# A decoder block on one core: orders of the FFN opening and of the last norm, and two held GpSimd splits

## What is computed

```python
for i in range(DEPTH):                      # DEPTH is 1
    a = rmsnorm(h, ln_mix[i])
    z = a @ w_in[i]                         # q, k, v, output gate, low-rank gate, u
    ...                                     # o: chunked gated linear attention, y_pool: trailing means
    mix = jnp.concatenate([o, y_pool], axis=-1) @ w_out[i]
    h = h + mix
    f = rmsnorm(h, ln_ffn[i])
    h = h + (jax.nn.silu(f @ w_ffn_gate[i]) * (f @ w_ffn_up[i])) @ w_ffn_down[i]
    e = rmsnorm(h, ln_ple[i])
    h = h + jax.nn.sigmoid(e @ w_ple_gate[i]) * (p[i].astype(h.dtype) @ w_ple_proj[i])
return rmsnorm(h, ln_final)
```

## Time and profile before

| | us |
|---|---|
| three timed runs | 1169.32, 1170.78 (median), 1171.07 |
| the profiled execution | 1169.47 |
| its span, first to last instruction | 1167.2 |
| TensorE busy | 1138.9 (98%) |
| VectorE, GpSimd, ScalarE busy | 642.6, 567.9, 405.5 |
| mean granted TensorE clock | 0.988 |

### The profile page before, as it was taken

The page is one execution under the profiler, slowest core; times in us unless marked ns, Lnnn a source line. Parts: engine busy times, 40 slices in busy tenths (PEclk is TensorE's granted clock), DMA queues, the critical chain, the costliest instruction groups (busy, mean ns, idle before and its releaser), DMA issues.

```text
span 1167.2 us, 15072 instructions
## 1 busy us (share of the span) xinstructions
PE 1138.9 (98%) x5614; PEld 943.4 (81%) x5614; DVE 642.6 (55%) x753; ACT 405.5 (35%) x635; POOL 567.9 (49%) x368
## 2 busy tenths in 40 slices
PE   9999999999999899999999999999999999999995
PEld 7788998777887688888888888888888888778884
DVE  7565576557548764445454545454545353884434
ACT  8402112164324442323233333333332332473422
POOL 0011275233226876656665656565656565782203
PEclk9999999999999999999999999999999999999997
DMA  6211111113001111111111111111111110401003
GB/s 246 90 36 37 37 38 37 36 73 144 37 1 36 54 56 54 54 54 54 54 54 54 54 54 54 54 54 54 54 54 54 54 54 18 180 1 45 10 1 144
DMA packets 23364, 67.94 MB, mean 58 GB/s; under 512 B 2528, under 2 KB 3616, under 8 KB 21408
## 3 DMA queue, kind: packets, MB, share of 16 engines
q1 hardware_dynamic: 23328, 67.44, 16.3%
HBM read 63.24 MB, written 4.19 MB: 58 GB/s over the span
## 4 chain that ended last, share of the span: by engine, by line
PE 36%; POOL 31%; issue 23%; DVE 5%; DMA 2%; ACT 1%; POOLq 1%; SPq 0%; DVEq 0%; ACTq 0%
POOL r_lo L553 18%; PE pb L1494 10%; PE pb L1495 10%; PE pb L1496 10%; POOL raw_b L571 4%; POOL raw_a L569 3%; POOL s_sum L564 2%; POOL raw_a L567 2%; PE pb L1621 2%; DVE t_raw L1307 1%; PE pb L1605 1%; POOL sums L613 1%; PE pb L1582 1%; DMA pp_raw<-in_w_ple_proj_dram 1%; PE pb L1567 1%
## 5 line engine op out<-in xcount | busy, mean ns | idle before, releaser
L1373 DVE TENSOR_TENSOR h<-h,pb 128x512 f32<-128x512 f32 x176 | 116.9, 682 | 51.9 <-PE pb L1496 50.8
L553 POOL TENSOR_TENSOR r_lo<-raw_b,r_hi 128x512 fp32r<-128x512 f32 x66 | 96.0, 1455 | 100.5 <-ACT r_hi L766 100.5
L489 POOL TENSOR_TENSOR w_lo<-w_raw,w_hi 128x2048 fp32r<-128x2048 f32 x10 | 49.8, 4981 | 183.1 <-ACT w_hi L630 183.1
L1717 PE MATMUL pb<-t_hi,r_hi 128*128 128x512 f32 x352 | 137.5, 391 | 0.0
L1718 PE MATMUL pb<-t_lo,r_hi 128*128 128x512 f32 x352 | 137.0, 389 | 0.0
L1719 PE MATMUL pb<-t_hi,r_lo 128*128 128x512 f32 x352 | 136.9, 389 | 0.0
L553 POOL TENSOR_TENSOR r_lo<-raw_a,r_hi 128x512 fp32r<-128x512 f32 x66 | 89.9, 1363 | 94.1 <-ACT r_hi L766 94.1
L1494 PE MATMUL pb<-gu_hi,r_hi 128*128 128x512 f32 x320 | 124.5, 389 | 0.0
L1495 PE MATMUL pb<-gu_lo,r_hi 128*128 128x512 f32 x320 | 124.5, 389 | 0.0
L1496 PE MATMUL pb<-gu_hi,r_lo 128*128 128x512 f32 x320 | 124.5, 389 | 0.0
L766 ACT CAST r_hi<-raw_b 128x512 fp32r<-128x512 f32 x66 | 41.0, 622 | 203.3 <-POOL raw_b L571 143.9
(11 more groups left out here) (219 smaller groups left out, 2627.7 us busy)
## 6 DMA issues: line engine op xcount, KB each, us to landing
raw_d<-in_w_ffn_down_dram SPq DMA_DIRECT2D x22, 512.0 KB, 3.5
w_raw<-in_w_in_dram SPq DMA_DIRECT2D x7, 1024.0 KB, 4.9
raw_a<-in_w_ffn_gate_dram SPq DMA_DIRECT2D x11, 512.0 KB, 3.4
raw_b<-in_w_ffn_gate_dram SPq DMA_DIRECT2D x11, 512.0 KB, 4.4
raw_a<-in_w_ffn_up_dram SPq DMA_DIRECT2D x11, 512.0 KB, 3.7
raw_b<-in_w_ffn_up_dram SPq DMA_DIRECT2D x11, 512.0 KB, 4.6
h<-in_x_t_dram SPq DMA_DIRECT2D x16, 256.0 KB, 6.0
w_raw<-in_w_out_dram SPq DMA_DIRECT2D x4, 1024.0 KB, 5.8
```

Of the source, the lines that this page charges most:

```text
L489: nc.gpsimd.tensor_tensor(w_lo[s][:, 0:size], w_raw[s][:, 0:size], w_hi[s][:, 0:size].bitcast(F32), ALU.subtract).then_inc(w_lo_ready[s], 1)
L553: nc.gpsimd.tensor_tensor(r_lo[q % RING][:].rearrange("p (k n) -> p k n", k=kts), src, r_hi[q % RING][:].bitcast(F32).rearrange("p (k n) - ...
L1373: V.tensor_tensor(h[:, m, both(c)], h[:, m, both(c)], aux.bank(F_DOWN + n)[:], ALU.add).then_inc(aux.drained, 1)
L1717: M(bank[:], wh[:, k, :], x_h[:, k, :], start=start and k == 0, stop=False, skip_group_check=True)
```

## The change

- **GpSimd in the output projection**: the split of the first w_out block now waits for four o_tok scalings, that of the second for eight o_low splits.
- **Buffers and loads of the opening**: the first up matrix is loaded as four quarters (`up21`, `up22`, `up11`, `up12`) in places of their own, three of them before the output projection ends. up21 and up22 lie where rms_all is, so VectorE's copies into rms_all wait for the 14th split.
- **Orders in the opening**, on ScalarE, GpSimd and VectorE. The spreading of the norm stands behind P9, one product earlier.
- **PLE**: GpSimd's first gate split waits for the last gu_lo; the casts and splits of the first w_ple_proj block and of p stand between the tiles of the e row.
- **Last norm**: the half 0 sums, root and spread stand inside the last two gate products; GpSimd multiplies m = 4 to 7 of half 0 and m = 6, 7 of half 1, from copies that ScalarE makes, VectorE the others from PSUM; TensorE does 14 matmuls of ones before the last sums and spreads half 1 to two banks; table loads of ScalarE are called ahead by dummy activations; the stores go in another order.

The core of the diff:

```diff
+        up21, up22 = (at(n, [P, HK, P], small[0] + o * KB) for n, o in (("up21", 0), ("up22", 2)))
...
             matrix_half(w_ffn_gate, 0, 1, raw_b, b_landed, (w_lo_ready[1], 5))
-            sp.wait_ge(ent_lo, 3)
-            matrix_half(w_ffn_up, 0, 0, raw_a0, a_landed, (proj.filled, U_OUT + 16))
-            matrix_half(w_ffn_up, 0, 1, raw_b0, b_landed, (proj.filled, U_OUT + 16))
+            def up_quarter(dst, half, right, landed):
+                part = w_ffn_up[0][:, half * HK * BW:(half + 1) * HK * BW].rearrange("p (k n) -> p k n", k=HK)
+                sp.dma_start(dst[:], part[:, :, right * P:(right + 1) * P]).then_inc(landed, 16)
+
+            sp.wait_ge(proj.drained, U_OUT)
+            up_quarter(up21, 0, 1, up2_landed)
+            up_quarter(up22, 1, 1, up2_landed)
+            sp.wait_ge(proj.filled, U_OUT + 12)
+            up_quarter(up11, 0, 0, up11_landed)
+            sp.wait_ge(proj.filled, U_OUT + 16)
+            up_quarter(up12, 1, 0, up12_landed)
             for i in range(1, GROUPS):
...
-            for c, normed in enumerate((y_first, y_second)):
-                for k in range(KT):
-                    sp.wait_ge(normed, k + 1)
+            for k in (0, 4, 1, 2, 5, 3, 6, 7):
+                sp.wait_ge(*((y_first, k + 1) if k < 4 else (y_first_pool, k - 3)))
+                sp.dma_start(out[k][:, both(0)], h[:, k, both(0)]).then_inc(out_stored, 16)
+            for c, normed in ((1, y_second),):
+                for k in (0, 1, 2, 3, 6, 4, 5, 7):
+                    sp.wait_ge(*((normed, k + 1) if k < 6 else (y_second_pool, k - 5)))
...
+            pool.wait_ge(o_scaled, 4)
             block_lo(NB)
...
+            pool.wait_ge(o_lo, 8)
             for b in range(NB + 1, NB + 4):
                 block_lo(b)
...
+            opening_lo(0)
+            pool.wait_ge(b_landed, 16)
+            opening_sum(0, 0)
+            opening_sum(0, 1)
+            opening_lo(1, 2)
+            opening_sum(0, 2)
+            opening_sum(0, 3)
+            opening_lo(3, 4)
+            pool.wait_ge(up2_landed, 32)
+            opening_sum(1, 0)
+            opening_sum(1, 1)
+            opening_sum(1, 2)
+            opening_lo(5, 6)
+            opening_sum(1, 3)
+            opening_lo(*range(7, D_FIRST))
             with pool.Fori(0, GROUPS - 1) as d:
...
+            pool.wait_ge(gu_lo_ready, 2 * GROUPS)
             gate_lo(0)
-            proj_lo(0)
-            pool.wait_ge(gu_ready, 2 * GROUPS)
...
             for n in range(16):
+                if n == 2:
+                    proj_lo(0)
+                if n in (4, 6):
+                    k = n // 2 - 2
+                    pool.wait_ge(p_hi_done, k + 1)
+                    nc.gpsimd.tensor_tensor(p_lo[:, k, :], p_raw[:, k, :], p_hi[:, k, :].bitcast(F32), ALU.subtract
+                                            ).then_inc(p_lo_done, 1)
...
-            pool.wait_ge(aux.drained, F_NORM4 + 2)
             pool.wait_ge(h_gained, 14)
-            for m in range(KT):
+            pool.wait_ge(spread_copied, 1)
+            for m in range(4, KT):
                 nc.gpsimd.tensor_tensor(h[:, m, both(0)], h[:, m, both(0)], rms_all[:, both(0)], ALU.mult
-                                        ).then_inc(y_first, 1)
+                                        ).then_inc(y_first_pool, 1)
+            pool.wait_ge(h_gained, 16)
+            pool.wait_ge(spread_copied, 2)
+            for m in range(6, KT):
+                nc.gpsimd.tensor_tensor(h[:, m, both(1)], h[:, m, both(1)], rms_all[:, both(1)], ALU.mult
+                                        ).then_inc(y_second_pool, 1)
...
-            proj_high(0, ent_lo, END + 4)
...
             for n in range(16):
+                if n == 2:
+                    proj_high(0, ent_lo, END + 4)
+                if n in (4, 6):
+                    k = n // 2 - 2
+                    act.wait_ge(p_landed, 16)
+                    act.wait_ge(aux.filled, F_NORM3 - 16)
+                    nc.scalar.copy(p_hi[:, k, :], p_raw[:, k, :]).then_inc(p_hi_done, 1)
...
+                if pair == 7:
+                    nc.scalar.activation(stat[:, 2, 1:2], ones[:, 0:1], ACT.Sqrt)
+                    root(3, 0)
+                    nc.scalar.activation(stat[:, 2, 2:3], ones[:, 0:1], ACT.Sigmoid)
                 for n in ns:
+                    if n == 15:
+                        act.wait_ge(aux.filled, F_NORM4 + 2)
+                        nc.scalar.copy(rms_all[:, both(0)], aux.bank(F_NORM4 + 1)[:]).then_inc(spread_copied, 1)
...
             root(3, 1)
+            act.wait_ge(aux.filled, F_NORM4 + NORM_FILLS + 1)
+            nc.scalar.copy(rms_all[:, both(1)], aux.bank(F_NORM4)[:]).then_inc(spread_copied, 1)
...
+                if pair == 7:
+                    norm_var(F_NORM4, 0)
+                    norm_diag(3, 0)
...
                     if n == 14:
-                        norm_var(F_NORM4, 0)
-                        norm_diag(3, 0)
-                if pair == 7:
-                    norm_take(F_NORM4, 0)
+                        dve.wait_ge(spread_copied, 1)
+                        dve.wait_ge(h_gained, 14)
+                        for m in range(4):
+                            i = V.tensor_tensor(h[:, m, both(0)], h[:, m, both(0)], aux.bank(F_NORM4 + 1)[:], ALU.mult
+                                                ).then_inc(y_first, 1)
...
-            for m in range(KT):
+            for m in range(6):
...
-                    if (mat, idx) == (0, 6):
+                    if (mat, idx) == (0, 5):
...
 
+            def last_sums(k):
+                if k == 5:
+                    token_sums(F_NORM4, 0, (y_sum, 14))
+
+            def last_spread(k):
+                if k == 3:
+                    spread_rms(F_NORM4, 3, 0)
+
...
             f = F_NORM4 + 2
+            aux.claim(f + 1)
+            for _ in range(LAST_ONES):
+                M(aux.bank(f + 1)[:, 0:P], ones[:], ones[:], start=True, stop=True)
             pe.wait_ge(y_sum, 15)
-            aux.claim(f)
+            pe.wait_ge(aux.drained, F_NORM4)
...
-            aux.claim(f + 1)
-            for t in range(4):
-                i = M(aux.bank(f + 1)[:, t * P:(t + 1) * P], stat[:, 3, 4 + t:5 + t].broadcast_to([P, P]), ident[:],
-                      start=True, stop=True)
-            i.then_inc(aux.filled, 1)
+            for bank in (aux.bank(f + 1), aux.bank(f + 2)):
+                for t in range(4):
+                    i = M(bank[:, t * P:(t + 1) * P], stat[:, 3, 4 + t:5 + t].broadcast_to([P, P]), ident[:],
+                          start=True, stop=True)
+                i.then_inc(aux.filled, 1)
```

162 lines of the change are left out of this document (84 added, 78 removed).

## The result

The changed kernel takes **1162.38 us** (median of four runs, 1161.71 to 1163.34), the kernel before in the same series 1170.92; ratio 0.9925, 95% interval 0.9911 to 0.9939. The forecast was 1156.6 with a range of 1152 to 1162: faster, as said, but 7.8 us by the profiled executions (1169.47 and 1161.71) instead of 14.2. Most of the difference arises in one place.

What follows compares the result with a forecast made beforehand. TensorE, busy 98% of the span, was taken as the bound, with 16 us of waits in four places. Gains of 2.3 + 7.0 + 0 + 4.9 = 14.2 turn 1169.47 into 1155.3, forecast as a 1156.6 median; range 1152 to 1162.

Steps and rivals of the forecast that it cites:

- Part 1: Output projection: o_tok scalings no longer blocked by GpSimd, part of the gain lost to later waits; 2.3 us gained.
- the one of 0.3: Output projection: second new TensorE wait, for an o_low split behind the second mix_lo instruction; 0.3 us.
- The lock rule: A GpSimd instruction blocks VectorE instructions with both sources in SBUF for its whole length; projection gain 2.3 us.
- a shared bandwidth: Alternative reading of GpSimd and VectorE sharing SBUF access in the output projection; the gain there would be 3.3 us.
- Part 2: FFN opening: three TensorE waits and slow clock go, smaller VectorE waits come; 7.0 us gained, bounds 2.5 and 10.4.
- a wait of 1.4 at the diagonal: FFN opening: TensorE waits 1.4 us for VectorE's diagonal product before spreading the norm.
- P17's weights are ready by 408.7 at the latest and wanted at 410.2: Fourth loop product: GpSimd's split delivers its weights before TensorE wants them, so no wait there.
- Part 3: Last down projection and PLE splits: 0 us, from -0.7 to +1.5.
- nothing: Last down projection: the wait for the last gu_lo moves the first gate split only from 1006.67 to 1006.96.
- Part 4: Last norm: fewer GpSimd multiplications, ones keeping the clock up, faster sums and spread; 4.9 us gained, bounds 1.2 and 5.5.
- opening slower: FFN opening: VectorE 1 to 3 us later, or clock down at P10; gain 9 to 12, about 1160; chance 0.24.
- slower than before: Around the first silu: casts, copies and GpSimd's sums all late behind one scaling, eating the 14 us; chance 0.06.

Runs made afterwards that it cites:

- o_lo_hold_off: The changed kernel without GpSimd's wait for the eighth o_low split ahead of its splits of w_out blocks 2 to 4; 1165.62 us.
- no_ones: The changed kernel without the 14 matmuls of ones before the last token sums; 1165.91 us.
- before_again: The kernel before, unchanged, in a second execution; 1169.28 us.
- gu_hold_off: The changed kernel without the one line that makes GpSimd's first PLE gate split wait for VectorE's last gu_lo split; 1168.96 us.
- gu_casts_later: The changed kernel with the two gu_hi casts of each loop pass moved on ScalarE behind the copies of the first two products; 1158.89 us.

## Why the forecast missed, part by part

**Part 1 was right**: 2.56 by A, forecast 2.3. The rows of the changed kernel, VectorE's first o_tok scalings and o_low splits, and TensorE's transposes and first w_out product:

```profile
252.95 2.50 DVE L1277 TENSOR_TENSOR o_tok<-o_tok,o_stat 128x512 f32<-128x512 f32 x4
...
262.89 4.16 DVE L1283 TENSOR_TENSOR mix_lo<-gated,mix_hi 128x512 fp32r<-128x512 f32 x4
...
256.96 1.91 PE L1653 MATMUL pb<-ident,o_tok 128*128 128x128 f32 x16
...
265.38 0.47 PE L1561 MATMUL pb<-mix_hi,w_hi 128*128 128x512 f32 x1 [1.03 <-DVE mix_lo L1283]
```

The scalings take 2.5 instead of 6.5, and the wait moved on to an o_low split is 1.03 (forecast 1.3); the one of 0.3 didn't come. The lock rule, which the Trainium skill ("SBUF — State Buffer", on the shared port pair) also has, gave the right size; a shared bandwidth would have given 3.3. One item was not in my list: an `o_stat` instruction of VectorE took 2.37 us under the split of the w_out block (0.16 before), so the first o_low split came up at 262.9, not 261.1, and took 2.35, not about 4. Both stand behind the same GpSimd instruction (260.07 to 264.69), so the sum did not feel it.

**Part 2 failed**: 0.8 instead of 7.0. Its first half stood nearly as forecast, P14 at 45.7 us behind P0 (44.7 forecast), no slow clock at P10 or P14. Of the missing 1.0, 0.6 lies ahead of P9 (0.2 of it a wait for a copy before P7) and 0.2 in the wait of P9, 1.6 for VectorE's up tile; I had looked for a wait of 1.4 at the diagonal, one product later. The step that broke is the last one: "P17's weights are ready by 408.7 at the latest and wanted at 410.2". The weights were ready at 408.9, but P17 needs a second thing, the bank of P15, and the copy that frees it stands on ScalarE behind the very casts that I had followed to get at the weights, and two gu_hi casts of 1.0 each. That cost 3.5 of wait and 1.7 of clock: of the 7.0 less 1.0, 0.8 was left. Before, the same queue stood there, but TensorE had lost 3.57 us at P14 and came so late that it never saw it: the copy of P15 ended at 416.4, and P17 started at 417.3. Two sizes were off as well: GpSimd's sums took 2.3 each, not 1.3 to 1.8, since VectorE's 1024-element instructions stood beside them (its products took 2.20 instead of 1.22). And there were more layers below: the copy of P18, then GpSimd. The price of the broken step is measured: mending ScalarE's order brings 4.5 us (B 65.56 against 70.08), to 5.3 under the kernel before; mending VectorE's and GpSimd's too brings 8.2. So the 7.0 was to be had, but not by this change.

**Part 3** was forecast at 0 with bounds of -0.7 and +1.5: measured -0.28. But the word "nothing" for its hold was wrong: the split moves by 0.3 only in an execution in which the gate's load lands late, and by 1.8 otherwise (in the changed kernel ScalarE's cast ends at 1001.7 and GpSimd begins at 1003.5).

**Part 4** was forecast at 4.9 and gave 4.2. Ones, sums, root and spread in the changed kernel, and the multiplications:

```profile
1145.19 3.29 PE L1901 MATMUL pb<-ones 128*128 128x128 f32 x28
1148.31 0.28 PE L1907 MATMUL pb<-ones,sums 128*128 128x1 f32 x2
...
1150.86 2.05 PE L1913 MATMUL pb<-ident,stat 128*128 128x128 f32 x16 [0.70 <-DVE stat L1549]
1152.06 3.67 DVE L1553 TENSOR_TENSOR h<-h,pb 128x512 f32<-128x512 f32 x6 [1.25 <-PE pb L1913]
...
1153.68 2.49 POOL L665 TENSOR_TENSOR h<-h,rms_all 128x512 f32<-128x512 f32 x2 [8.68 <-ACT rms_all L1013]
```

Each term stood: 3.1 for the ones (3.0), 1.8 for the sums (1.7), 2.05 for both spreads (2.2), the last multiplication 10.8 behind the last weight matmul's end (11). The missing 0.7 is behind it: the span ended 3.5 later, not 2.8, by the last stores.

The rival *opening slower* was nearest (a gain of 9 to 12), but its mechanism, VectorE late or the clock down at P10, was not the one. The rival *slower than before* came closest in kind: it names the queue behind one scaling, GpSimd's sums and the copies. I gave it too little, because I asked when it would eat all 14 us, not what it would take of the 7.

## What to carry to other kernels

When a stall goes, list for each of the next products everything that it waits for (weights, operand, bank) and who frees each; a queue that was hidden by the stall comes out at its full length. A copy that frees a bank should never stand on its engine behind an instruction that waits for a slower engine or a load. And where GpSimd and VectorE both read SBUF, the order of one is a cost of the other: a hold on the one off the path pays, but look at what then follows at once on the held instruction (o_lo_hold_off: 5.6 us).

## What the runs showed of the hardware

The same wait does not always cost the same clock. The wait of 3.5 us before P17 left a granted clock of 0.62 in the changed kernel, 0.50 in no_ones (B 1.3 longer, with nothing changed there) and 1.00 in o_lo_hold_off (B 1.5 shorter). The 3.4 before the last down projection left 1.00 in before_again and 0.50 in gu_hold_off. Behind the waits of 1.6 before P17 in gu_casts_later and before P9 in no_ones it was 1.00. Shorter waits divide as well: 2.35 before the first transposes of the kernel before left 1.00, 2.32 before the last sums of no_ones left 0.50, and so did 0.6 and 1.9 close together in the opening of the kernel before (0.66 in the window of the earlier trace rows). What decides between them I could not read from these traces, and it stays open; for a sum it means that the wait of 3.5 us before P17 cost its length and between 0.2 and 3.0 us more (0.2 in o_lo_hold_off, 1.7 in the changed kernel, 3.0 in no_ones).

The lock works in both directions: GpSimd's 512-element instruction takes 1.29 alone and 2.28 beside VectorE's 1024-element one, which takes 1.22 alone and 2.20 beside it.
